# Three float32r matmuls a k tile: the two with the high weights as one 512-column matmul, their halves added later on VectorE

## The reference, cut to what matters

```python
proj = rmsnorm(x, norm_g) @ w_in              # 2048 x 7184; w_out 2048 x 2048
q = rmsnorm(x) @ w_xq; kv = rmsnorm(mem) @ w_xkv; o @ w_xo
gate = causal_dwconv(h @ w_gate, conv_w) + conv_b
x = x + (silu(gate) * (h @ w_up)) @ w_down    # 2048 x 5632 x 2, 5632 x 2048
zxbcdt = x @ a_w_in                           # 2048 x 10304; then conv, silu, SSD
x = layernorm(ALPHA * x + y @ a_w_out)
k, v = split(x @ kv_w + kv_b)                 # 2048 x 512
q, gate = split(x @ b_w_in)                   # 2048 x 4096; q + bias, rope, windowed attention
x = layernorm(ALPHA * x + (o * silu(gate)) @ b_w_out)
```

## Time and profile before

| what | value |
|---|---|
| median of 3 runs | 2501.78 us |
| the runs | 2472.42, 2501.78, 2502.83 us |
| span of the profiled execution | 2471.0 us, granted TensorE clock 0.998 |
| PE, VectorE, ScalarE, GpSimd busy | 99%, 70%, 49%, 18% |
| DMA | 418 MB, mean 169 GB/s |

### The profile page before, as it was taken

How to read it: one execution, slowest core, us unless ns; L and a number is a source line. 1 busy time by engine, 2 the same in 40 slices (tenths; PEclk the granted TensorE clock), 3 DMA queues, 4 the chain that set the end, 5 groups by cost and what they waited for, 6 DMA issues and landing times.

```text
span 2471.0 us, 51530 instructions
## 1 busy us (share of the span) xinstructions
PE 2434.6 (99%) x20866; PEld 2376.3 (96%) x20866; DVE 1727.8 (70%) x2768; ACT 1220.4 (49%) x1918; POOL 437.7 (18%) x535
## 2 busy tenths in 40 slices
PE   7999999999999999999999999999999999999998
PEld 7999999999999999999999999999999999899998
DVE  6677646685666656665657877777787778777777
ACT  5434334554544444444444545444445554566554
POOL 1233310160200000000003201330101112511002
PEclk9999999999999999999999999999999999999999
DMA  6433335565455556556556654454454445444453
GB/s 220 158 124 120 127 126 180 189 200 171 155 196 193 193 176 212 197 176 212 195 174 190 195 167 157 161 179 156 156 189 153 158 158 183 151 154 144 149 163 118
DMA packets 124501, 418.34 MB, mean 169 GB/s; under 512 B 13796, under 2 KB 17644, under 8 KB 124012
## 3 DMA queue, kind: packets, MB, share of 16 engines
q1 hardware_dynamic: 124268, 415.06, 51.1%
HBM read 412.37 MB, written 3.68 MB: 168 GB/s over the span
## 4 chain that ended last, share of the span: by engine, by line
PE 93%; DVE 3%; POOL 2%; issue 1%; ACT 1%; DMA 0%; SPq 0%; ACTq 0%; POOLq 0%; DVEq 0%
PE b L766 27%; PE b L767 27%; PE b L768 27%; PE b L744 2%; PE b L1109 1%; DVE WL L1647 1%; PE b L887 1%; DVE t1s L1745 1%; PE b L900 1%; PE b L1120 1%; PE b L737 1%; POOL t1s L2547 0%; PE b L1175 0%; POOL ACC L2378 0%; PE b L1214 0%
## 5 line engine op out<-in xcount | busy, mean ns | idle before, releaser
L766 PE MATMUL b<-XH,WH 128*128 128x256 f32 x4224 | 1196.5, 283 | 18.2 <-DVE WL L1647 14.6
L768 PE MATMUL b<-XH,WL 128*128 128x256 f32 x4224 | 1173.5, 278 | 0.0
L767 PE MATMUL b<-XL,WH 128*128 128x256 f32 x4224 | 1173.4, 278 | 0.0
L1236 ACT ACTIVATE WH<-WR 128x1024 fp32r<-128x1024 f32 (+2 forms) x811 | 817.6, 1012 | 505.0 <-PE b L768 500.3
L1647 DVE TENSOR_TENSOR WL<-WR,WH 128x1024 fp32r<-128x1024 f32 (+2 forms) x811 | 984.5, 1223 | 14.9 <-ACT WH L1236 14.7
L766 PEld LDWEIGHTS b<-XH,WH 128*128 128x128 f32 x4224 | 795.7, 188 | 30.4 <-issue 14.2
L767 PEld LDWEIGHTS b<-XL,WH 128*128 128x128 f32 x4224 | 795.8, 188 | 3.0 <-issue 2.4
L768 PEld LDWEIGHTS b<-XH,WL 128*128 128x128 f32 x4224 | 797.0, 189 | 0.0
L766 PE MATMUL b<-OH,WH 128*128 128x256 f32 x1680 | 472.9, 282 | 2.9 <-DVE WL L1647 2.4
L768 PE MATMUL b<-OH,WL 128*128 128x256 f32 x1680 | 466.6, 278 | 0.0
L767 PE MATMUL b<-OL,WH 128*128 128x256 f32 x1680 | 466.5, 278 | 0.0
(11 more groups left out here) (397 smaller groups left out, 2241.5 us busy)
## 6 DMA issues: line engine op xcount, KB each, us to landing
WR<-a_w_in SPq DMA_DIRECT2D x160, 512.0 KB, 3.7
WR<-w_in SPq DMA_DIRECT2D x112, 512.0 KB, 3.6
WR<-w_gate SPq DMA_DIRECT2D x88, 512.0 KB, 3.8
WR<-w_up SPq DMA_DIRECT2D x88, 512.0 KB, 4.2
WR<-a_w_out SPq DMA_DIRECT2D x64, 512.0 KB, 3.5
WR<-b_w_in SPq DMA_DIRECT2D x64, 512.0 KB, 3.5
WR<-w_down SPq DMA_DIRECT2D x64, 384.0 KB, 3.5
WR<-w_down SPq DMA_DIRECT2D x64, 320.0 KB, 2.9
```

The lines of the kernel that those rows point to most:

```text
L766: mm(ps, WH[:, slot, at:at + P], xh, start=(k == 0), stop=False)
L767: mm(ps, WH[:, slot, at:at + P], xl, start=False, stop=False)
L768: m = mm(ps, WL[:, slot, at:at + P], xh, start=False, stop=(k == p["kt"] - 1))
L1236: act.activation(WH[:, s, 0:n], WR[:, r, 0:n], ACT.Copy).then_inc(*act_w.up(i))
```

## The change

For nine kinds of product (`HALVES`: all but those that add into XT) the two matmuls with the high weights become one of 512 columns. Its moving operand is the high and the low x side by side, its output a whole bank: columns 0 to 255 the product with the high x (and, added by the third matmul, low weights by high x), columns 256 to 511 the product with the low x. For that XH and XL become two halves of one tensor XX, OH and OL of OO.

The two halves of the bank are added after the product: ScalarE copies columns 256 to 511 into `lop` right after the product (`lowhalf`), VectorE adds columns 0 to 255 to it, waits for its own result, and does the old operation with `low` in place of `ps` (for swq and bkv one operation does both). VectorE's part, and all that followed it, is emitted ahead of the second half of the next product's chunk instead of at the product's end (`waiting`, `add_up`); the steps `convA`, `gateA`, `kvt` and those of `xat` are shifted by a slot to go with it. `wg`'s tanh on ScalarE reads `lop` after the addition.

To make room, the one-hot table (384 columns) leaves the constants and is loaded by a DMA of its own at the start, and the positions are loaded when `rot` begins instead of at the start.

```diff
@@ class Plan
 def drain(self, left=0):
+    if not left:
+        self.add_up()
     while self.evacs or len(self.small) > left:
         self.slot()
@@ def product: between the halves of a chunk
     self.step("half", key, i, k0, k0 + 4, k0, False)
     self.slot()
     self.more(i)
+    self.add_up()
     self.step("half", key, i, k0 + 4, k1, k0, True)
@@
 def evac(self, key, p):
+    if p["evac"] in HALVES:
+        self.step("lowhalf", key)
     if self.held_back is not None:
         self.held_back.append((key, p))
         return
+    self.add_up()
+    if p["evac"] in HALVES:
+        self.waiting = (key, p)
+    else:
+        self.evacuate(key, p)
+
+def add_up(self):
+    if self.waiting is not None:
+        what, self.waiting = self.waiting, None
+        self.evacuate(*what)
+
+def evacuate(self, key, p):
     self.step("evac", key)
...
-    self.evacs.append((key, [None, "convA", "gateA", "cB"] if ... else [None, "gateA", "cB"]))
+    self.evacs.append((key, ["convA", "gateA", "cB"] if ... else ["gateA", "cB"]))
@@ TensorE, half_of
+two = banks[p["bank"]][:, :].rearrange("p (h t) -> p h t", h=2)
...
-    mm(ps, WH[:, slot, at:at + P], xh, start=(k == 0), stop=False)
-    mm(ps, WH[:, slot, at:at + P], xl, start=False, stop=False)
-    m = mm(ps, WL[:, slot, at:at + P], xh, start=False, stop=(k == p["kt"] - 1))
+    if p["evac"] in HALVES:
+        mm(two, WH[:, slot, at:at + P], x, start=(k == 0), stop=False)
+    else:
+        mm(ps, WH[:, slot, at:at + P], x[:, 0, :], start=(k == 0), stop=False)
+        mm(ps, WH[:, slot, at:at + P], x[:, 1, :], start=False, stop=False)
+    m = mm(ps, WL[:, slot, at:at + P], x[:, 0, :], start=False, stop=(k == p["kt"] - 1))
@@ ScalarE
+def low_half(key):
+    b = plan.products[key]["bank"]
+    w.wait_ge(*pe_prod.of(key))
+    act.activation(lop[:, b, :], banks[b][:, S:2 * S], ACT.Copy).then_inc(*act_lo.up(key))
@@ VectorE, evac
 w.wait_ge(*pe_prod.of(key))
+if kind in HALVES:
+    low = lop[:, p["bank"], :]
+    w.wait_ge(*act_lo.of(key))
+    if kind not in ("swq", "bkv"):
+        dve.tensor_tensor(low, ps, low, ALU.add).then_inc(*dve_lo.up(key))
+        w.wait_ge(*dve_lo.of(key))
 if kind == "conv":
...
-    dve.tensor_tensor(cvs[...], ps, RB[:, :], ALU.mult)
+    dve.tensor_tensor(cvs[...], low, RB[:, :], ALU.mult)
@@ SyncE
-    sp.dma_start(posb[:, :], d["positions"])
+    sp.dma_start(T2(16)[0:33, 0:384], d["onehot"])
...
+def rot(name):
+    if name == "a":
+        w.wait_ge(*pe_ssm.of("nr", 6))
+        w.wait_ge(*act_os.of("ssm", 27))
+        sp.dma_start(T2(1)[:, 0:S].bitcast(I32), d["positions"])
```

More of the change, by code:

```diff
@@ L32 @@
     ("ident", 128), ("U", 128), ("L", 128), ("lev", 7 * 128), ("ones", 128),
-    ("caus", 128), ("prev", 128), ("caus2", 128), ("rot", 128), ("invf", 1), ("onehot", 384), ("mhalf", 16),
+    ("caus", 128), ("prev", 128), ("caus2", 128), ("rot", 128), ("invf", 1), ("mhalf", 16),
 ]
@@ L87, in constants @@
     oh[32] = n < 0
-    put("onehot", oh)
-    return c
+    return c, oh.astype(np.float32)
 class Signal:
@@ L178, in __init__ @@
         self.held_back = None
+        self.waiting = None
         self.lows = []
@@ L357, in norm @@
         self.begin(("norm", v), ["sums", "rows"], gap, first)
+HALVES = ("conv", "gate", "plain", "kv", "xq", "up", "bkv", "swg", "swq")
 VERSION = {("wo", 1): 1, ("dn", 3): 3}
@@ L757, in half_of @@
             for k in range(k0, k1):
-                xh, xl, by = moving(key, k)
+                x, by = moving(key, k)
                 if by[0] == "x":
@@ L1484, in evac @@
                 ti = key[1]
-                w.wait_ge(*pe_prod.of(key))
+                w.wait_ge(*dve_lo.of(key))
                 if ti:
                     w.wait_ge(*dve_ev.of(("wg", ti - 1)))
-                act.activation(T1(8), banks[plan.products[key]["bank"]][:, 0:S], ACT.Tanh, scale=0.5).then_inc(
+                act.activation(T1(8), lop[:, plan.products[key]["bank"], :], ACT.Tanh, scale=0.5).then_inc(
                     *act_swa.up("th", ti))
@@ L1629, in scalar @@
                 "convA": conv_a, "gateA": gate_a, "gdn": gdn, "att": att, "mem": mem, "kvt": kvt, "xat": xat,
-                "evac": evac, "two": two, "time": time, "ssm": ssm, "rot": rot, "mid": mid, "ln": ln, "vd": vd, "swa": swa}
+                "evac": evac, "lowhalf": low_half, "two": two, "time": time, "ssm": ssm, "rot": rot, "mid": mid, "ln": ln, "vd": vd, "swa": swa}
         for kind, *what in plan.steps:
@@ L1839, in evac @@
                 if m < 4:
-                    dve.tensor_tensor(KM[:, m, :], ps, T1(6), ALU.mult).then_inc(*dve_ev.up(key))
+                    dve.tensor_tensor(KM[:, m, :], low, T1(6), ALU.mult).then_inc(*dve_ev.up(key))
                 else:
@@ L1857, in evac @@
                 w.wait_ge(*pe_ln.of("cols", 0))
-                dve.tensor_scalar(T1(m), ps, pc("kv_b", m), None, ALU.add).then_inc(*dve_ev.up(key))
+                dve.scalar_tensor_tensor(T1(m), ps, pc("kv_b", m), low, ALU.add, ALU.add).then_inc(*dve_ev.up(key))
             elif kind == "swg":
@@ L1866, in evac @@
                     w.wait_ge(*act_os.of("swa", ti - 4))
-                dve.scalar_tensor_tensor(T1(ti % 4), T1(8), 1.0, ps, ALU.add, ALU.mult).then_inc(*dve_ev.up(key))
+                dve.scalar_tensor_tensor(T1(ti % 4), T1(8), 1.0, low, ALU.add, ALU.mult).then_inc(*dve_ev.up(key))
             elif kind == "swq":
@@ L1872, in evac @@
                     w.wait_ge(*pe_swa.of("rope", ti - 2))
-                dve.tensor_scalar(T1(4 + ti % 2), ps, pc("q_b", ti), None, ALU.add).then_inc(*dve_ev.up(key))
+                dve.scalar_tensor_tensor(T1(4 + ti % 2), ps, pc("q_b", ti), low, ALU.add, ALU.add).then_inc(*dve_ev.up(key))
         def two(m):
@@ L2709, in finish @@
             w.wait_ge(*st_tb.of("t"))
-        does = {"start": start, "issue": issue, "toep": toep, "att": att, "mem": mem, "kd": kd,
+        does = {"start": start, "issue": issue, "toep": toep, "att": att, "mem": mem, "rot": rot, "kd": kd,
                 "finish": finish}
@@ L2781, in lay @@
     o["params"] = np.ascontiguousarray(np.concatenate([p[n] for n, _ in PARAMS], axis=1))
-    o["consts"] = constants()
+    o["consts"], o["onehot"] = constants()
     o["rel"] = np.concatenate([a["rel_bias"], np.full((1, 8), NEG, np.float32)])
```

49 lines of the change are left out of this document (26 added, 23 removed).

## The result

The changed kernel takes 2557.82 us (four runs, 2556.18 to 2559.1) against 2487.1 for the kernel before (2471.07, 2472.42, 2501.78, 2502.83 in the runs beside it, so that the median lies between two levels): ratio 1.0268, interval 1.0204 to 1.0332. It is slower; the forecast was 2466, the range 2432 to 2500.

A forecast was written before the change was run, and what follows sets the result against it. The prediction took TensorE's matmul stream as the bound. From the median 2501.8 us it took off 41.7 for the merged matmuls and added 6 for VectorE's addition: 2466 us, range 2432 to 2500.

The forecast's parts named there:

- The merged matmul: In 272 products ending in SBUF, 4352 k tiles each lose one matmul and one weight load: 35.4 us saved, bounds 0 and 58.
- the fixed piece: Time beside a matmul's bare columns, taken as fixed per instruction: 6.67 ns saved per merged k tile, 11.1 at the slower spacing.
- the sum of 35.4 us: Saving on the profiled execution: 4352 k tiles at 6.67 ns, 29.0 us, plus 6.4 for the third at the slower spacing.
- The straight line: fp32 matmuls of 128, 256 and 512 columns, 273, 378 and 591 ns: only bare columns, 0.82 to 0.83 ns each, grow with length.
- nothing is won: Lower bound of the merger: if the 6.6 ns belong to the columns, 512 columns cost 2 x 113.3 ns, saving 0.
- A: Rival for the merged matmul: the piece is mostly the columns', so only 10 us saved, 2498 us; chance 20%.
- The two spacings: TensorE's 256-column matmuls start every 113.3 or about 117.8 ns; over the feed-forward stretch the slower costs 28 us more.
- ScalarE's copy: 272 copies of 256 columns from PSUM at 365 ns, 99 us, falling into ScalarE's wait for PE; nothing on the path.
- VectorE's addition: An added 0.42 us PSUM operation after most merged products, 106 us on VectorE, paid for by waits for PE that go.
- The +6 of its effect: Delay by the addition: 4 us in gdn, ssm and swa chains, 1.6 where results are wanted at once; bounds 0 and 30.
- Rival D: VectorE becomes the bound outside the feed-forward stretch, at the low halves WL (line 1647): 74 us, 2534; chance 5%.
- The loads: Smaller constants up to 1 us earlier at the start, later positions load between -1 and +3 us; 0 taken for both.

The follow-up runs named there:

- split_halves: Changed kernel with its 512-column matmul taken apart again into two of 256, layout, copies, additions and order kept: 2543.02 us, runs from 2515.95 to 2548.67.
- merge_alone: Kernel before with only the 512-column matmul and joint x layout; no copy, no addition, old order, high-weights-by-low-x product left out of the result: 2517.04 us.
- late_copy: Changed kernel with ScalarE's copy emitted behind the small tasks of the slot in place of ahead of them: 2554.55 us.
- add_at_once: Changed kernel with copy, addition and evacuation all at the product's end and small steps in the old order, merged matmul kept: 2533.48 us.
- m3_scan: TensorE alone, three-matmul and merged streams at 32 shifts of the moving operand, behind four and six small matmuls: least k tile 340 ns old form, 346.0 merged.
- m2_places: TensorE alone, first scan of operand shifts, also shorter weights and columns: at shift 48 three matmuls took 353.3 or 340.0 ns a k tile, merged 353.3.
- m1_streams: TensorE alone, five streams of old form, merged form and single lengths: merged k tile 353.2 ns in two pieces, old form 360.0 in four of five.

## Why the prediction was wrong

*What bounds the kernel.* Right: TensorE's stream, and everything followed from its distances.

*The merged matmul.* The step that failed is "I take 6.67, the fixed piece", and with it the sum of 35.4 us. It took the piece measured on the three-matmul stream at its best, gave the merged matmul the same, and counted one less. But the time beside the columns is no constant of the instruction. A k tile has 320 ns of bare columns; in the scan three matmuls add 20 to 40 ns to them and two add 26 to 34, by the operand's place, and at 48, this kernel's place, it is 20.0 or 33.3 for three and 33.3 for two. The straight line of the earlier trace rows is fp32 at two cycles a column and says nothing of a stream at one. Its bound was wrong as well: "nothing is won" as the worst case took the k tile's own spacing as given, 340 for 340. Merged it is 353.3, a loss of 13.3 ns on each k tile that was at 340. No rival had the merged form slower; A, which gave most of the piece to the columns, still forecast a gain of 10 us.

*The two spacings.* They were seen, priced (13.3 ns) and taken as the reason for the spread of the runs: the kernel before has runs at 2469 to 2475 and at 2500 to 2503, and split_halves spreads as widely. That fits, but no run at 2502 was profiled, so it is not shown. The forecast also rests on it: it starts from 2501.8, a level at which the kernel before ran in 2 of its 4 runs beside the changed one and in the minority later. But the spacings were taken as a draw that the change leaves alone (a third stays at the slower). They are a property of addresses and of phase, that is of what ran just before, and the form of the stream is part of it: at this shift the merged form has almost only the slower spacing. It also carries over: in the feed-forward stretch the down products, still three matmuls a k tile, were all at 340 and are all at 353. In all +44 us, merge_alone.

*ScalarE's copy.* Its size was right (379 for 365 ns) and so was that its own wait hurts nothing (late_copy).

*VectorE's addition.* Its size was right, 420 ns and 106 us. The +6 of its effect, bounds 0 and 30, was mis-sized: 41 us between merge_alone and the changed kernel. I had asked what the addition delays and gave each chain 0.1 to 0.2 us; copies and additions are 16 us even in the old order (add_at_once). What I didn't price at all is the moved order: "the pair is now issued four k tiles after" was counted as a gain only, the waits for PE that go. VectorE's waits for PE at these lines did go, and 103.8 us of waits for `lop` came in their place. But the taps, ScalarE's tanh and the low halves moved along and came to stand ahead of steps of ssm and gdn for which PE waits: 15.5 us by the order alone. Nor was it priced that TensorE's clock falls behind some of these waits: 5.5 at least of the 9 us by which order and operations together exceed their sum. Rival D named the engine and the direction, with the wrong place: it isn't WL (PE waited 17.0 us for it before and 19.4 after, nearly all at the start), but the small operations.

*The loads.* The wait for the positions was 4.8 us on VectorE, once, with no stall of that length on PE behind it. Nothing, as taken.

The account, from the medians: 2472.9 before, +44.2 for the merged form's spacing, +16.4 for copies and additions, +24.3 for the moved order on top of them, the falls of the clock included: 2557.8. The forecast started from 2501.8, the other level of the kernel before: against that the change lost 56 us, against 2472.9 it lost 85.

## What to carry to other kernels

When a stream of matmuls is the bound, find its distance from start to start and what sets it before pricing a change of its form; a bound of "as now" is none when the distance has more than one level. Here the levels hang on where the moving operand lies, and 192 bytes were worth 90 us, as much as the whole loss of the change. So a form is not good or bad by itself: this one was the faster at most places of the scan and lost where it was tried. The form and the place are to be tried together. A step that is moved in a hand-written order takes along all that is chained to it, and each must be held against the small operations that it now stands ahead of. A wait that looks short by itself can cost again in the clock behind it.

## What the runs showed of the hardware that was not expected

- The float32r stream's k tile of 768 columns took 340.0 to 360.1 ns as three matmuls and 346.0 to 354.1 as two (m3_scan), at the 2.4 GHz level, depending on the shift of the moving operand (period 256 bytes) and, at some shifts, on what ran just before it. In the feed-forward stretch of the kernel before one spacing lasted throughout, 714 us.
- Weights of 16 columns in place of 128 left the three-matmul k tile at 353.3 and took 3.7 ns off the merged one (m2_places).
- 128 float32r columns alone started every 111.7 ns, 256 every 117.8 (m2_places), 384 every 173.5 and 512 every 227.4 (m1_streams): under 256 columns a shorter matmul bought almost nothing.
- The Trainium skill, "TensorE: Matmul & The Clock Gate", section "Back-to-back issue gap", gives N / 2.4 + 2.5 ns, which is 109.2 for 256 columns and 215.8 for 512, and calls it the gap of an isolated matmul. In these streams the runs show 113.3 at best and 120 at worst, and 227.4 and 235: the measurement decides, and the rule has no term for the place.
- GpSimd and VectorE cost one another time when both work on SBUF operands, and who pays changes with what meets: GpSimd's product of 256 columns (L2463 before, L2499 after) took 738 ns by itself and 1657 where the new order puts it beside a low half of VectorE:

```profile
L2463 POOL TENSOR_TENSOR t2s<-t2s,RB x44: 733/738/741, 667.6 to 1254.6; 128x256 f32<-128x256 f32 x44
```
```profile
L2499 POOL TENSOR_TENSOR t2s<-t2s,RB x44: 1382/1657/1662, 691.4 to 1301.7; 128x256 f32<-128x256 f32 x44
```

The first is the source view of the kernel before (min/median/max ns), the second of the changed one. In the timeline of the latter the two lie beside each other, and the low half keeps its 1.22 us. GpSimd's product runs 0.61 us past the low half's end, most of its 738 ns, so (an estimate from these rows) it makes little headway beside it:

```profile
725.14 1.22 DVE L1677 TENSOR_TENSOR WL<-WR,WH 128x1024 fp32r<-128x1024 f32 x1
725.31 1.66 POOL L2499 TENSOR_TENSOR t2s<-t2s,RB 128x256 f32<-128x256 f32 x1 [9.61 <-DVE t2s L1803]
```

That product stood off the path there. The taps of gdn, above, did not: they are the case in which VectorE paid, 3.21 us for 1.53.
